# Start of a three-block transformer kernel: x, the first norm and the parameter columns in one block by tiles, and token slots zeroed by GpSimd

## The reference, cut to what matters

```python
def rmsnorm(x, g):
    xf = x.astype(jnp.float32)
    y = xf * lax.rsqrt(jnp.mean(xf * xf, axis=-1, keepdims=True) + EPS)
    return (y * g.astype(jnp.float32)).astype(x.dtype)
...
x = first_block(x, ...)     # begins with rmsnorm(x, norm_mix_pre) @ w_in
x = second_block(x, ...)
return third_block(x, ...)  # ends with hierarchical_moe: two experts for each token
```

## Time and profile before

| | |
|---|---|
| median of 3 runs | 3475.6 us (3475.31 to 3475.69) |
| the profiled execution, its time | 3475.73 us |
| span of its trace | 3474.1 us |
| PE busy | 3127.3 us (90%) |
| DVE busy | 1247.2 us (36%) |
| ACT busy | 654.8 us (19%) |
| POOL busy | 123.1 us (4%) |
| TensorE's granted clock, mean | 0.94 of full |
| zeroing `x_slots`, 2 transfers | 8448 KB each, 45.2 us (median) to landing |
| first product (L176) starts | 60.63 us |

### The profile page before, as it was taken

How to read it: one execution, slowest core, us unless ns; L and a number is a source line. 1 busy time by engine, 2 the same in 40 slices (tenths; PEclk the granted TensorE clock), 3 DMA queues, 4 the chain that set the end, 5 groups by cost and what they waited for, 6 DMA issues and landing times. The chain is left out here.

```text
span 3474.1 us, 36324 instructions
## 1 busy us (share of the span) xinstructions
PE 3127.3 (90%) x14114; PEld 1993.5 (57%) x14114; DVE 1247.2 (36%) x2365; ACT 654.8 (19%) x1497; POOL 123.1 (4%) x147
## 2 busy tenths in 40 slices
PE   3969998999999889896999999898959996899997
PEld 2447775884458654584478854686745764333332
DVE  1354433320033565146153301333664133233334
ACT  0021112220010450281011000112541022111111
POOL 1000000000000200001000000000010001000000
PEclk9979999999999989897999999898959997999998
DMA  8211221212222102200223221222001303999995
GB/s 307 97 49 49 73 79 49 97 73 79 82 65 97 49 1 73 74 2 12 73 73 97 73 91 54 88 73 97 1 21 53 121 15 152 423 423 424 424 423 231
DMA packets 128060, 420.33 MB, mean 121 GB/s; under 512 B 6545, under 2 KB 35618, under 8 KB 107442
## 3 DMA queue, kind: packets, MB, share of 16 engines
q1 hardware_dynamic: 112496, 379.37, 28.4%
q10 hardware_dynamic: 10546, 23.70, 1.9%
q0 software_dynamic: 4880, 15.35, 1.3%
HBM read 394.81 MB, written 23.59 MB: 120 GB/s over the span
## 5 line engine op out<-in xcount | busy, mean ns | idle before, releaser
L750 PE MATMUL bank<-arena 128*128 128x256 f32 x4480 | 980.6, 382 | 6.1 <-PEq L131 3.2
L750 PEld LDWEIGHTS bank<-arena 128*128 128x128 f32 x4480 | 858.5, 192 | 130.8 <-issue 12.5
L423 PE MATMUL bank<-arena 128*128 128x512 f32 x1504 | 658.1, 600 | 10.3 <-PEq L932 5.3
L423 PEld LDWEIGHTS bank<-arena 128*128 128x128 f32 x1504 | 288.6, 193 | 373.1 <-issue 373.1
L176 PE MATMUL bank<-arena 128*128 128x512 f32 (+9 forms) x1384 | 458.0, 490 | 43.2 <-PEq L2709 11.5
L176 PEld LDWEIGHTS bank<-arena 128*128 128x128 f32 (+3 forms) x1384 | 245.9, 196 | 250.2 <-issue 225.8
L3149 DVE TENSOR_TENSOR arena<-arena,bank 128x512 f32<-128x512 f32 x128 | 87.7, 687 | 139.2 <-PE bank L3053 136.9
L497 DVE SCALAR_TENSOR_TENSOR arena<-arena,bank 128x512 f32<-128x512 f32 x32 | 20.6, 683 | 311.9 <-PE bank L423 311.9
L3053 PE MATMUL bank<-arena 128*128 128x512 f32 x256 | 123.0, 615 | 4.4 <-DVE arena L3135 4.4
L3025 PE MATMUL bank<-arena 128*32 128x512 f32 x1024 | 115.7, 594 | 11.1 <-DMA arena<-in_moe_w_up_dram 11.1
L187 PE MATMUL bank<-ident,arena 128*128 128x128 f32 (+3 forms) x202 | 35.3, 349 | 92.1 <-PEq L1030 36.8
(11 more groups left out here) (466 smaller groups left out, 3170.2 us busy)
## 6 DMA issues: line engine op xcount, KB each, us to landing
arena<-in_moe_w_gate_dram SPq DMA_DIRECT2D x64, 1024.0 KB, 16.5
arena<-in_moe_w_up_dram SPq DMA_DIRECT2D x64, 1024.0 KB, 18.7
arena<-in_moe_w_down_dram SPq DMA_DIRECT2D x32, 2048.0 KB, 24.0
arena<-in_w_in_dram SPq DMA_DIRECT2D x29, 2048.0 KB, 7.8
arena<-in_w_ff_dram SPq DMA_DIRECT2D x16, 2048.0 KB, 8.3
x_slots<-zeros ACTq DMA_DIRECT2D x2, 8448.0 KB, 45.2
arena<-in_w_out_dram SPq DMA_DIRECT2D x8, 2048.0 KB, 7.9
arena<-in_w_gate_dram SPq DMA_DIRECT2D x11, 1024.0 KB, 5.3
```

The lines of the kernel that those rows point to most:

```text
L423: last = pe.matmul(c.banks[2 * i + half][:, :], hidden[:, k0 + k, i * P:(i + 1) * P], w[:, k, half * 512:(half + 1) * 512], start=k0 + k = ...
L750: last = pe.matmul(bank[:, m, :], lhsT, rhs, start=fresh and m == 0 and k == 0, stop=k == 3, skip_group_check=True)
```

## The change

The block of `setup_constants` now also loads x in four transfers by tile, takes sums of squares, roots and scalings tile by tile, transposes the tiles and the parameters and empties the banks. The parameter transfers move from ScalarE's queue to SyncE's, between x and the weights. `clear_slots` is called on GpSimd in the same block: it zeroes unit 9 (128 x 4096) and, once the parameter columns are copied, issues nine transfers (eight of 2 MB, one of 512 KB) in which every partition writes up to 16 KB in one piece. GpSimd waits for them at the end of `tables`. The blocks of `inverse_rms`, `scale_rows`, `to_features`, of the parameter columns and of `clear_slots` go away here.

```diff
@@ -985,58 +985,97 @@
             moves.append((rows[n][at:at + count, :], src.rearrange("(r p) -> r p", p=P)))
             c.col[name] = c.columns[n][:, at:at + count]
             at += count
+    normed, gain = c.region(6, 0, NT, D), c.col["norm_mix_pre"]
+    inv, junk = c.small[:, 100:104], c.region(8, 0, D)
+    x_loaded = [c.sig(f"x_loaded{i}") for i in range(NT)]
+    squared, mean, root, order, scaled, turned, columns_turned, columns_ready, emptied = (c.sig(n) for n in (
+        "squares_summed", "mean_ready", "root_ready", "vector_order", "rows_scaled", "rows_turned", "columns_turned",
+        "columns_ready", "bank_emptied_by_vector"))
+    banks = [c.banks[n] for n in (0, 1, 2, 3, 4, 5, 7, 6)]
     with nc.Block() as block:
         @block.gpsimd
         def _(pool):
+            pool.memset(rows[0][:, :], 0.0).then_inc(made.sem, made.up())
+            pool.memset(rows[1][:, :], 0.0).then_inc(made.sem, made.up())
             pool.memset(c.ident[:, :], 0.0).then_inc(made.sem, made.up())
             pool.memset(c.keep_le[:, :], 0.0).then_inc(made.sem, made.up())
-            pool.memset(c.ones[:, :], 1.0).then_inc(made.sem, made.up())
-            pool.memset(c.region(11, 0, 256), 0.0).then_inc(made.sem, made.up())
             pool.wait_ge(made.sem, made.at(4))
             pool.affine_select(out=c.ident[:, :], in_=c.ident[:, :], compare_op=ALU.not_equal, fill=1.0,
                                         base=0, pattern=[[-1, P]], channel_multiplier=1).then_inc(set_.sem, set_.up())
             pool.affine_select(out=c.keep_le[:, :], in_=c.keep_le[:, :], compare_op=ALU.is_ge, fill=NEG,
                                         base=0, pattern=[[-1, P]], channel_multiplier=1).then_inc(set_.sem, set_.up())
-            pool.wait_ge(set_.sem, set_.at(2))
+            pool.memset(c.ones[:, :], 1.0).then_inc(set_.sem, set_.up())
+            pool.wait_ge(set_.sem, set_.at(3))
+            clear_slots(c, pool, columns_ready)
+
+        @block.sync
+        def _(sync):
+            for i in range(NT):
+                sync.dma_start(c.x[:, i, :], a["x"][0, i * P:(i + 1) * P, :]).then_inc(x_loaded[i].sem, x_loaded[i].up(16))
+            sync.wait_ge(made.sem, made.at(2))
+            for dst, src in moves:
+                sync.dma_start(dst, src).then_inc(loaded.sem, loaded.up(16))
+            c.load_weights(sync)
 
         @block.scalar
         def _(act):
-            act.wait_ge(made.sem, made.at(4))
-            for dst, src in moves:
-                act.dma_start(dst, src).then_inc(loaded.sem, loaded.up(16))
-            act.wait_ge(loaded.sem, loaded.at(16 * len(moves)))
-
-        @block.sync
-        def _(sync):
-            x = a["x"][0].rearrange("(i p) d -> p i d", p=P)
-            loaded_x = c.sig("x_loaded")
-            sync.dma_start(c.x, x).then_inc(loaded_x.sem, loaded_x.up(16))
-            sync.wait_ge(loaded_x.sem, loaded_x.at(16))
-            sync.wait_ge(loaded.sem, loaded.at(16 * len(moves)))
-            c.load_weights(sync)
-    bank_groups(c, [((), turns(c, [rows[n]]), (), "v", copy_to(c.columns[n][:, :])) for n in range(2)])
+            for i in range(NT + 1):
+                if i < NT:
+                    act.wait_ge(x_loaded[i].sem, x_loaded[i].at(16))
+                    if i:
+                        act.wait_ge(squared.sem, squared.at(i))
+                    act.activation(junk, c.x[:, i, :], ACT.Square,
+                                   accum_out=inv[:, i:i + 1]).then_inc(squared.sem, squared.up())
+                if i:
+                    act.wait_ge(mean.sem, mean.at(i))
+                    act.activation(inv[:, i - 1:i], inv[:, i - 1:i], ACT.Sqrt).then_inc(root.sem, root.up())
+
+        @block.vector
+        def _(dve):
+            for i in range(NT + 1):
+                if i < NT:
+                    dve.wait_ge(squared.sem, squared.at(i + 1))
+                    dve.tensor_scalar(inv[:, i:i + 1], inv[:, i:i + 1], 1.0 / D, EPS1, ALU.mult,
+                                      ALU.add).then_inc(mean.sem, mean.up())
+                if i:
+                    dve.wait_ge(root.sem, root.at(i))
+                    dve.reciprocal(inv[:, i - 1:i], inv[:, i - 1:i]).then_inc(order.sem, order.up())
+                    dve.wait_ge(order.sem, order.at(i))
+                    dve.tensor_scalar(normed[:, i - 1, :], c.x[:, i - 1, :], inv[:, i - 1:i], None,
+                                      ALU.mult).then_inc(scaled.sem, scaled.up())
+            dve.wait_ge(columns_turned.sem, columns_turned.at(1))
+            for n in range(2):
+                dve.tensor_copy(c.columns[n][:, :], c.banks[6][:, n * P:(n + 1) * P]).then_inc(columns_ready.sem,
+                                                                                               columns_ready.up())
+            dve.wait_ge(columns_ready.sem, columns_ready.at(2))
+            for n in range(2 * NT):
+                i, k = n // 2, 4 * (n % 2)
+                dve.wait_ge(turned.sem, turned.at(n + 1))
+                dve.tensor_tensor(c.xT[:, k:k + 4, i * P:(i + 1) * P], banks[n][:, :].rearrange("p (k t) -> p k t", k=4),
+                                  gain[:, k:k + 4].unsqueeze(2).to_broadcast([P, 4, P]),
+                                  ALU.mult).then_inc(emptied.sem, emptied.up())
+
+        @block.tensor
+        def _(pe):
+            pe.wait_ge(set_.sem, set_.at(1))
+            for n in range(2 * NT):
+                i, k = n // 2, 4 * (n % 2)
+                pe.wait_ge(scaled.sem, scaled.at(i + 1))
+                if n == 2 * NT - 2:
+                    pe.wait_ge(loaded.sem, loaded.at(16 * len(moves)))
+                    for m in range(2):
+                        last = pe.transpose(c.banks[6][:, m * P:(m + 1) * P], rows[m], c.ident[:, :])
+                    last.then_inc(columns_turned.sem, columns_turned.up())
+                if n == 2 * NT - 1:
+                    pe.wait_ge(columns_ready.sem, columns_ready.at(2))
+                for j in range(4):
+                    last = pe.transpose(banks[n][:, j * P:(j + 1) * P], normed[:, i, (k + j) * P:(k + j + 1) * P],
+                                        c.ident[:, :])
+                last.then_inc(turned.sem, turned.up())
 
 
 def first_block(c, a):
     nc, x, xT = c.nc, c.x, c.xT
-    small = c.small
-
-    normed = c.region(6, 0, NT, D)
-    row_inverse = small[:, 100:104]
-    inverse_rms(c, [x[:, i, :] for i in range(NT)], EPS1, c.region(8, 0, D), row_inverse)
-
-    def scale_rows(dst, src, inv, n=NT):
-        done = c.sig("rows_scaled")
-        with nc.Block() as block:
-            @block.vector
-            def _(dve):
-                for i in range(n):
-                    dve.tensor_scalar(dst(i), src(i), inv(i), None, ALU.mult).then_inc(done.sem, done.up())
-                dve.wait_ge(done.sem, done.at(n))
-    scale_rows(lambda i: normed[:, i, :], lambda i: x[:, i, :], lambda i: row_inverse[:, i:i + 1])
-    to_features(c, lambda i: normed[:, i, :], xT, c.col["norm_mix_pre"])
-
-
     latents = c.region(7, 0, NT, 416)
     gating = c.region(7, 1664, NT, 512)
     convpool = c.region(6, 0, 8, S)
@@ -1071,6 +1110,7 @@
         pool.affine_select(out=ws, in_=ws, compare_op=ALU.is_ge, fill=0.0, base=0,
                            pattern=[[0, 4], [-1, P]], channel_multiplier=1).then_inc(picked.sem, picked.up())
         pool.wait_ge(picked.sem, picked.at(1))
+        pool.wait_ge(c.signals["slots_cleared"].sem, c.signals["slots_cleared"].sent)
     groups = []
     for n, key in enumerate(("conv", "pool")):
         w = c.slot(key)[0]
@@ -2624,23 +2664,18 @@
 MAX_PAIRS = 32
 
 
-def clear_slots(c):
-
-    zeros = c.sb("zeros", [P, 512])
+def clear_slots(c, pool, parameters):
+
+    zeros = c.region(9, 0, UNIT)
+    made, cleared = c.sig("zeros_made"), c.sig("slots_cleared")
     c.x_slots = c.nc.dram_tensor("x_slots", ((MAX_PAIRS + 1) * PAIR, D), F32).ap()
-    made, cleared = c.sig("iota_made"), c.sig("slots_cleared")
-    with c.nc.Block() as block:
-        @block.gpsimd
-        def _(pool):
-            pool.memset(zeros[:, :], 0.0).then_inc(made.sem, made.up())
-
-        @block.scalar
-        def _(act):
-            act.wait_ge(made.sem, made.at(1))
-            for half in range(2):
-                dst = c.x_slots[:, half * 512:(half + 1) * 512].rearrange("(b p) n -> p b n", p=P)
-                act.dma_start(dst, zeros[:, :].unsqueeze(1).to_broadcast([P, MAX_PAIRS + 1,
-                                                                          512])).then_inc(cleared.sem, cleared.up(16))
+    room = c.x_slots.rearrange("(p r) n -> p (r n)", p=P)
+    pool.memset(zeros, 0.0).then_inc(made.sem, made.up())
+    pool.wait_ge(made.sem, made.at(1))
+    pool.wait_ge(parameters.sem, parameters.at(2))
+    for at in range(0, room.shape[1], UNIT):
+        n = min(UNIT, room.shape[1] - at)
+        pool.dma_start(room[:, at:at + n], zeros[:, 0:n]).then_inc(cleared.sem, cleared.up(16))
 
 
```

(1 more changed line is left out.)

## The result

| | before | changed |
|---|---|---|
| median of 8 runs | 3475.83 us (3475.31 to 3478.02) | 3487.4 us (3484.94 to 3488.94) |
| profiled execution, its span | 3475.73, 3474.1 us | 3488.94, 3487.3 us |
| first product starts | 60.63 us | 67.50 us |
| granted clock, mean | 0.940 | 0.931 |

The ratio is 1.0031, interval 1.0020 to 1.0042: slower, by a little more than such a measurement can tell. The profile's own execution is at the upper end of its runs, 13.2 us of span above the one before.

What follows compares the result with a forecast made beforehand. TensorE's idle start, with ScalarE's queue blocked and whole-tile steps, was the bound. First product from 60.63 to 21.4 gains 39.2 us, less 1.2 for the clock: 38.0, median 3475.6 to 3437.6 us; range 3434 to 3446.

Steps and rivals of the forecast that it cites:

- The bound: Start of the kernel: TensorE idles until 60.63 us behind whole-tile steps and ScalarE's queue, held 23.49 us by zeroing issues.
- parts 1 to 3: First block: x loaded by tiles, squares and roots by tile, then transposes, columns and xT; first product at 21.4 us.
- the sum: First product from 60.63 to 21.4 us: 39.2 gained, less 1.2 for the clock, 38.0; median 3437.6 us.
- rows 4: Earlier profile rows: Sqrt at 554.08 followed by Square at 557.22 without a load; so one extra table load counted.
- the table rival: ScalarE, first block: Square needs its own table, four more loads, 5.1 us, time 3442.7; chance 0.04.
- Part 4: Zeroing on GpSimd, first block: nine issues take 4.9 us, to 20.9, hidden by VectorE; zeros flow beside the first products.
- The cover I named: Block of first products: ends near 128, GpSimd's wait for zeros and small loads near 75, some 50 us of cover.
- GpSimd's queue fills up: First block: GpSimd holds only some transfers, last issue waits 20.5 us; block ends near 41, time 3457; chance 0.09.
- The zeros hold the block of the first products: End of that block: GpSimd waits for slow zeros; at 100 GB/s 37 us slower than before, 3513; chance 0.03.
- Zeros crowd out weights: DMA queues: 16 KB zero packets starve weights; `pool` at 45 costs nothing, at 63.3 gives 3452; stall chance 0.06.
- Part 5: Clock before the first product: TensorE waits 4.6 us for VectorE; loss between 0 and 2.4 us, taken as 1.2.
- every later stage keeps its length: After the block of first products, ending near 128 to 130: every stage at its old length.

Runs made afterwards that it cites:

- e1: The changed kernel with all nine zeroing transfers issued by GpSimd in the next block, behind `tables`' 14 loads; 3442.43 us, ratio 0.9899 to the kernel before.
- e2: As e1, but the first of the nine zeroing transfers (2 MB) stays in the first block; 3448.12 us, ratio 0.9915 to the kernel before.
- e7: e1 plus 28 useless identity transposes on TensorE while VectorE empties the banks; 3439.1 us, ratio 0.9889 to the kernel before.
- e8: e7 plus the two parameter transposes moved ahead of x's tile 2; 3438.09 us, ratio 0.9889 to the kernel before.
- e5: The kernel before with its two zeroing transfers issued by GpSimd instead of ScalarE, all else kept; 3507.86 us, ratio 1.0088.
- e4: The changed kernel with the nine zeroing transfers issued by SyncE behind three weight chunks in the first block; 3444.17 us, ratio 0.9899 to the kernel before.

## Why the prediction was wrong

**The bound and parts 1 to 3 held.** ScalarE's blocked queue and the chain of whole-tile steps were together worth what was said: with nothing but the zeroing moved, e1 has its first product at 20.11 where the sum had 21.4. How the gain divides between the two, which I put at 24 us and the rest, no run tested. The steps ran ahead of the sum by 0.4 us at first and 1.1 at the end: Square 0 at 4.88 for 5.3, the last scaling done at 13.0 for 13.9, xT at 19.97 for 21.1. The chain had one table load, as rows 4 said (another, at 0.91, ended before x was there); the table rival is out, and its price would have been 5.1. One reading was wrong without harm: the pace of the transposes didn't double in the earlier trace rows, since 11 in 2.00 us and 11 in 1.26 are a factor of 1.6.

**Part 4 failed, in one sentence:** "The nine issues start at 16.0 and stand on the block's end, because every engine leaves the block together." The issues were priced rightly (4.90 us for 4.9) and the block's end was seen. What was left out is that GpSimd does not reach that end when it has issued, but when its transfers have landed. So the 42 us of zeros, which part 4 let "flow beside the first products", stood on the path: the end is 67.2 and not 21.1. The term read 0 and measured 46.9 us (67.50 against 20.6, when the issues were done). My own figure for the zeros' end, "about 66", was right, and it was the block's end. The cover I named (50 us of products) could not start.

The rivals came near and missed. "GpSimd's queue fills up" had the right engine and block, but a wrong cause and half the price (20.5 us of delay for 47); e2 excludes it. "The zeros hold the block of the first products" had the right kind of wait one block too late. No rival asked what else, besides a semaphore wait, an engine does at a block's end. The view by line lists each queue's DRAIN, and I didn't read it for the kernel before. There GpSimd waits for its transfers by semaphore ahead of every block's end that I read, so no DRAIN of it stood behind one in flight. The DRAIN that did is ScalarE's, right behind its two zeroing transfers (view by line of L2632, kernel before):

```profile
L2632 ACTq DRAIN  x1: 153/153/153, 41.1 to 41.1; - x1
```

It took 0.15 us, and the zeros landed until 76.7. So the trace before could have raised the question, but for GpSimd it had no answer, and by ScalarE's example it pointed the other way.

"Zeros crowd out weights" was right in its mechanism. In the changed kernel the queues from 25 to 40 us show (packets, MB, share):

```profile
q0 software_dynamic: 395, 5.69, 88.5%
q1 hardware_dynamic: 399, 0.70, 12.0%
```

The counts are equal, as with packets taken in turn, at a mean of 14.4 KB for zeros against 1.75 for weights, and `latents` took 56.9 us to land. Its price of nothing was not put to the test, because the block's end held the products for longer. `pool` landed at 32.8 us, where the rival had 45, and would have been needed at about 48, so as an estimate it would have cost nothing. The Trainium skill ("DMA: Bandwidth & Descriptors", Queues, rings and completion order) lets a DMA engine finish a packet before it turns to another queue; the equal counts agree with it.

**Part 5 was under-sized.** It took 1.2 us for the clock. In e1 the pause costs 1.5 us at the first products, as e7 shows. The profiled execution of e1, the fastest of its four at 3437.22, has its first product 40.5 us earlier and its end 38.5: 1.5 at the first products and 0.5 in all later stages. The other three took 3442.2 to 3443.1, 5 to 6 us more, and their traces are not here, so where the median's 35.1 loses the rest is open. In other traces it is in later stages whose clock falls in a pause and comes back after a different time. Around one such pause the kernel before and the changed one read:

```profile
2024.00:2027.00 3.00, 2.45 (x3) 1.17 (x4) 0.00 (x0) 1.28 (x1) 0.00 (x0) 0.52 0.92 380
2027.00:2030.00 3.00, 3.00 (x8) 1.32 (x7) 0.00 (x0) 0.00 (x0) 0.00 (x0) 0.91 1.03 371
```

```profile
2034.00:2037.00 3.00, 2.48 (x3) 1.18 (x4) 0.00 (x0) 1.28 (x1) 0.00 (x0) 0.50 0.96 388
2037.00:2040.00 3.00, 3.00 (x5) 1.24 (x4) 0.00 (x0) 0.00 (x0) 0.00 (x0) 0.50 1.03 351
```

The same products after the same pause: eight in the second window before, five after the change. In the changed kernel VectorE's first step behind them (L497) comes 11.57 us later than before, where the one ahead of them came 9.96 later: 1.6 us lost. The profiled changed kernel is 6.9 us late at the first product and 13.2 at the end; 1.84 of the difference arise at the first products (8.98 us to the first full bank, against 7.14), 1.6 here, the rest in pieces below 1.5 at other pauses, some of them gains. I had written that every later stage keeps its length; none of the instructions changed, and still some did not. What decides how long the clock takes to return I didn't settle. It does not average out in the medians of e1 and of the changed kernel, which are 3.9 and 2.9 us above what the first product and its pause explain.

Would e1 have been inside the forecast? Its 3442.4 is, and the forecast of 3437.6 lies 0.5 from e8's. The second is luck: e8 has two edits that the sum did not have, and its chain is 1.6 us faster than the sum's 21.4. The sum described a kernel that the change was not.

## What to carry to other kernels

Before a transfer is hidden behind the next block, ask how its issuing engine leaves this one. A transfer issued by GpSimd has to land inside its block (all those tried here write from the core's memory to DRAM; loads were not tried), so put it into the block that is long enough to hide it, or issue it from SyncE or ScalarE and count the time for which that queue is held. When all engines wait for a block's end, read each queue's DRAIN in the view by line: the one that ends last names the engine, and what ends with it, an instruction or a landing, is what it waited for.

## What the runs showed of the hardware

- GpSimd's DRAIN at a block's end lasted until its own transfers had landed: 0.05, 10.9, 26.0, 47.9 us for none, one and four of 2 MB and for all nine, and 53.5 us with two of 8448 KB in e5. SyncE's took 0.12 us in e4 at 26.2 us, with all nine of its transfers still to land, and ScalarE's 0.15 us in the kernel before. The Trainium skill ("DMA: Bandwidth & Descriptors", Issuing engines are not separate DMA queues) says that transfers started on several engines at once save only the sequencer's time to initiate them; here the choice of the engine also decided when the block could end, and the measurement stands.
- The time for which a queue is held by issuing is its own quantity: 17.3 MB took ScalarE 23.49 us in two issues of 2 KB rows, GpSimd 3.8 us in two (e5) and 4.9 in nine, SyncE 12.8 in nine behind 5.9 MB of weights.
- The granted clock fell to its lower level 4.0 us (e1) into a pause in which VectorE alone worked, and 28 transposes of no other use kept it at the upper one (e7). They won 1.5 us at the first products and put 0.07 between the last emptying and the first product.
